# First layer of a hybrid decoder trunk: weight rests of three input units on GpSimd, convolution tap matrices on ScalarE, 12 instead of 15 taps per channel chunk on TensorE

## What is computed

```python
h = rms_norm(x, mix_norm[layer])
z = h @ ab_w_in[j]                       # 1024 x 2560
q, k, v, u = jnp.split(z, [512, 1024, 1536], axis=-1)
a = diff_attention(q, k, v, ...)         # 4 heads, two softmaxes each, their difference weights v
c = conformer_conv(u, ...)               # GLU, causal depthwise convolution of width 31 over 512 channels,
                                         # group norm over 64 channels, swish
x = x + jnp.concatenate([a, c], axis=-1) @ ab_w_out[j]
...
# in conformer_conv
val, gate = jnp.split(u, 2, axis=-1)
g = val * jax.nn.sigmoid(gate)
y = lax.conv_general_dilated(g, dw[:, None, :], window_strides=(1,), padding=[(30, 0)], ...) + dw_bias
```

## Time and profile before

| | before |
|---|---|
| median of 3 runs | 1492.41 us |
| the profiled execution: its time | 1492.52 us |
| the profiled execution: its span | 1490.4 us |
| TensorE busy | 1463.7 us (98%) |
| VectorE busy | 1208.6 us (81%) |
| ScalarE busy | 995.7 us (67%) |
| GpSimd busy | 132.8 us (9%) |
| granted TensorE clock, mean | 0.998 |

### The profile page before, as it was taken

One profiled execution on the slowest core, in us unless ns is written; L12 is line 12 of the kernel. 1 busy time (PEld: TensorE's weight loads), 2 busy tenths in 40 slices (PEclk: granted clock), 3 DMA queues, 4 the chain that ended last, 5 costly groups with the idle time before them and its releaser, 6 DMA issues.

```text
span 1490.4 us, 19624 instructions
## 1 busy us (share of the span) xinstructions
PE 1463.7 (98%) x7818; PEld 1237.3 (83%) x7818; DVE 1208.6 (81%) x1031; ACT 995.7 (67%) x850; POOL 132.8 (9%) x201
## 2 busy tenths in 40 slices
PE   8999999999999999999999999999999999999998
PEld 7967888889998778888888888888888888888776
DVE  7976766666386799888888888888888888888997
ACT  5667444465546677777777777777777777777774
POOL 8505200000253000000000000000000000000200
PEclk9999999999999999999999999999999999999999
DMA  9504555546510399999999999999999999999994
GB/s 344 171 6 164 197 197 181 185 143 197 193 34 31 116 349 372 352 387 379 348 377 382 351 374 388 365 362 386 374 349 389 377 349 380 381 347 377 411 377 164
DMA packets 206919, 432.50 MB, mean 290 GB/s; under 512 B 6914, under 2 KB 56251, under 8 KB 206827
## 3 DMA queue, kind: packets, MB, share of 16 engines
q1 hardware_dynamic: 204880, 424.78, 78.2%
q0 software_dynamic: 1904, 6.46, 1.1%
q10 hardware_dynamic: 42, 0.01, 0.0%
HBM read 426.51 MB, written 4.72 MB: 289 GB/s over the span
## 4 chain that ended last, share of the span: by engine, by line
PE 92%; DVE 4%; ACT 2%; issue 1%; DMA 0%; DVEq 0%; SPq 0%; ACTq 0%
PE bank L1466 25%; PE bank L1468 25%; PE bank L1467 25%; PE bank L1507 6%; PE bank L1509 3%; PE bank L1739 2%; PE bank L1868 2%; PE bank L1820 1%; DVE w_l L294 1%; PE bank L1720 1%; DMA raw<-in_ab_w_in 0%; PE bank L1721 0%; ACT w_h L289 0%; PE bank L1567 0%; PE bank L1473 0%
## 5 line engine op out<-in xcount | busy, mean ns | idle before, releaser
L294 DVE TENSOR_TENSOR w_l<-raw,w_h 128x2048 fp32r<-128x2048 f32 x402 | 920.8, 2292 | 182.1 <-ACT w_h L289 181.4
L289 ACT ACTIVATE w_h<-raw 128x2048 fp32r<-128x2048 f32 x402 | 770.9, 1918 | 353.3 <-PE bank L1468 287.4
L1466 PE MATMUL bank<-w_h,hs_h 128*128 128x512 f32 x896 | 355.3, 397 | 3.7 <-DVE w_l L294 2.8
L1468 PE MATMUL bank<-w_h,hs_l 128*128 128x512 f32 x896 | 349.7, 390 | 0.0
L1467 PE MATMUL bank<-w_l,hs_h 128*128 128x512 f32 x896 | 349.0, 390 | 0.0
L1466 PEld LDWEIGHTS bank<-w_h,hs_h 128*128 128x128 f32 x896 | 168.3, 188 | 38.1 <-issue 3.3
L1468 PEld LDWEIGHTS bank<-w_h,hs_l 128*128 128x128 f32 x896 | 168.2, 188 | 36.0
L1467 PEld LDWEIGHTS bank<-w_l,hs_h 128*128 128x128 f32 x896 | 168.5, 188 | 33.2
L1466 PE MATMUL bank<-w_h,ma_h 128*128 128x512 f32 x448 | 174.6, 390 | 1.7 <-DVE w_l L294 1.7
L1467 PE MATMUL bank<-w_l,ma_h 128*128 128x512 f32 x448 | 174.3, 389 | 0.0
L1468 PE MATMUL bank<-w_h,ma_l 128*128 128x512 f32 x448 | 174.3, 389 | 0.0
(11 more groups left out here) (298 smaller groups left out, 1661.1 us busy)
## 6 DMA issues: line engine op xcount, KB each, us to landing
raw<-in_moe_w_in SPq DMA_DIRECT2D x224, 1024.0 KB, 5.7
raw<-in_moe_w_out SPq DMA_DIRECT2D x112, 1024.0 KB, 5.4
raw<-in_ffn_w_in SPq DMA_DIRECT2D x22, 1024.0 KB, 5.0
raw<-in_hgrn_w_in SPq DMA_DIRECT2D x16, 1024.0 KB, 5.1
raw<-in_ffn_w_out SPq DMA_DIRECT2D x11, 1024.0 KB, 4.7
raw<-in_ab_w_in SPq DMA_DIRECT2D x10, 1024.0 KB, 11.3
raw<-in_ab_w_out SPq DMA_DIRECT2D x4, 1024.0 KB, 4.8
raw<-in_hgrn_w_out SPq DMA_DIRECT2D x4, 1024.0 KB, 4.9
```

Of the source, the lines that this page charges most:

```text
L289: act.activation(w_h[:, u0 % S, :], raw[:, u0 % R, :], ACT.Copy).then_inc(w_high, 1)
L294: eng.tensor_tensor(w_l[:, u0 % S, :], raw[:, u0 % R, :], w_h[:, u0 % S, :], ALU.subtract).then_inc(w_low, 1)
L1466: pe.matmul(o, a_high, b_high, start=start, stop=False, skip_group_check=True)
L1468: return pe.matmul(o, a_low, b_high, start=False, stop=stop, skip_group_check=True)
```

## The change

It does five things, all in the first layer.

- GpSimd makes no tap matrices. It makes the rests of units 5, 7 and 9 (`POOL_UNITS`) with a semaphore of its own, `w_pool`; VectorE makes the rest of the following unit after it has waited for GpSimd's, and counts both.
- ScalarE makes the tap matrices, now 24, in four goes of six behind the high parts of units 4 to 7.
- PE_TAPS is 12: TensorE has 12 taps for each chunk of pair 1, VectorE 19.
- VectorE has 7 steps of taps ahead of the point where units 5, 7 and 9 stood and 4 elsewhere, taps 0 to 6 of pair 1 ahead of the norms of queries and keys, taps 6 to 8 behind the lambda steps, none within the softmax, and 8 to 19 behind it.
- TensorE has 14 taps ahead of the transposes (22 before), 3 ahead of the mean products (none before) and 7 behind (8 before).

```diff
-PE_TAPS = 15
+PE_TAPS = 12
+POOL_UNITS = (5, 7, 9)
...
+            if isinstance(u0, int) and isinstance(rounds, int) and rounds == 0 and u0 in POOL_UNITS:
+                eng.wait_ge(w_pool, POOL_UNITS.index(u0) + 1)
+            else:
+                eng.wait_ge(w_low, u0 + 1 + R * rounds)
...
+        def split_pool(pool, u0):
+
+            pool.wait_ge(w_high, u0 + 1)
+            pool.tensor_tensor(w_l[:, u0 % S, :], raw[:, u0 % R, :], w_h[:, u0 % S, :], ALU.subtract).then_inc(w_pool, 1)
+
+        def split_after_pool(dve, u0):
+
+            dve.wait_ge(w_pool, POOL_UNITS.index(u0 - 1) + 1)
+            dve.wait_ge(w_high, u0 + 1)
+            dve.tensor_tensor(w_l[:, u0 % S, :], raw[:, u0 % R, :], w_h[:, u0 % S, :], ALU.subtract).then_inc(w_low, 2)
...
-            pool.wait_ge(par_cp, 2)
-            for c in range(2):
-                for k in range(PE_TAPS):
-                    col = (TAPS - PE_TAPS + k) * 4 + 2 + c
-                    pool.tensor_scalar(diag(c * PE_TAPS + k), ident[:], dw[:, col:col + 1], None, ALU.mult).then_inc(c_diag, 1)
+            for u in POOL_UNITS:
+                split_pool(pool, u)
...
-            for u in range(4, N_AB_IN + 1):
-                conv_taps(0, 4 * (u - 4), min(4 * (u - 3), TAPS))
-                split_low(dve, u)
+            at = 0
+            for u in range(4, N_AB_IN):
+                more = 7 if u in POOL_UNITS else 4
+                conv_taps(0, at, min(at + more, TAPS))
+                at += more
                 if u == 5:
                     conv_value(1)
-            conv_taps(0, 28, TAPS)
-            conv_taps(1, 0, 2)
+                if u - 1 in POOL_UNITS:
+                    split_after_pool(dve, u)
+                elif u not in POOL_UNITS:
+                    split_low(dve, u)
+            conv_taps(1, 0, 4)
+            split_after_pool(dve, N_AB_IN)
+            conv_taps(1, 4, 6)
...
+            conv_taps(1, 6, 8)
+
...
             row_max(1)
-            conv_taps(1, 2, 4)
             row_max(2)
-            conv_taps(1, 4, 6)
             row_max(3)
             weights(0, p_0)
             row_max(4)
             row_max(5)
-            conv_taps(1, 6, 8)
...
+            def tap_matrices(n0, n1):
+
+                act.wait_ge(par_cp, 2)
+                for n in range(n0, n1):
+                    col = (TAPS - PE_TAPS + n % PE_TAPS) * 4 + 2 + n // PE_TAPS
+                    act.activation(diag(n), ident[:], ACT.Copy, scale=dw[:, col:col + 1]).then_inc(c_diag, 1)
...
                 split_high(act, u + 3)
+                if 1 <= u <= 4:
+                    tap_matrices(6 * (u - 1), 6 * u)
...
-            conv_part(1, 0, 7)
+            conv_part(1, 0, 2)
...
+            conv_part(1, 2, 5)
             for b in range(2):
                 pe.wait_ge(a_sq, b + 1)
...
-            conv_part(1, 7, PE_TAPS).then_inc(c_pe, 1)
+            conv_part(1, 5, PE_TAPS).then_inc(c_pe, 1)
```

More of the change, by code:

```diff
@@ L183, in build @@
         w_high, w_used = sem("w_high"), sem("w_used")
-        w_low = sem("w_low")
+        w_low, w_pool = sem("w_low"), sem("w_pool")
         x_in = [sem(f"x_in{tt}") for tt in range(TT)]
@@ L241, in wait_split @@
         def wait_split(eng, u0, rounds=0):
-            eng.wait_ge(w_low, u0 + 1 + R * rounds)
+            if isinstance(u0, int) and isinstance(rounds, int) and rounds == 0 and u0 in POOL_UNITS:
+                eng.wait_ge(w_pool, POOL_UNITS.index(u0) + 1)
+            else:
+                eng.wait_ge(w_low, u0 + 1 + R * rounds)
         def level_of(t, g, li):
```

## The result

| | before | changed |
|---|---|---|
| median of the runs | 1492.41 us (1492.30 to 1493.67, 5 runs) | 1500.71 us (1498.17 to 1507.72, 5 runs) |
| profiled execution | 1492.52 us | 1498.17 us |
| span | 1490.4 us | 1496.4 us |
| mean granted clock | 0.998 | 0.997 |

The ratio is 1.0053, 95% interval 1.0037 to 1.0069: slower by 0.5%. In the profiled executions the change costs 5.65 us, in the medians 8.3. The prediction of 1496.9 had the sign right and the range of 1491.7 to 1499.0 did not reach 1500.71.

What follows compares the result with a forecast made beforehand. TensorE, without gaps from 112 us on, carries earlier changes to the end; before that VectorE has next to nothing to spare. +7.0 - 0.3 - 3.6 + 1.3 = +4.4 us gave 1496.9 us, range 1491.7 to 1499.0.

Steps and rivals of the forecast that it cites:

- The bound: From 112 us on TensorE has no gaps, so any gain or loss before that carries to the end one for one.
- Step 1, the matrices: Tap matrices on ScalarE cost 0; taking them off GpSimd gives VectorE back 1.2 us.
- Step 2, the block: GpSimd's rests of units 5, 7, 9 spare VectorE 6.8 us but block its taps 3.9 each, +11.7.
- Side by side: Rival: GpSimd's long subtractions do not hold VectorE's second input; -0.4 us, 1492.1; chance 0.28 including a short block.
- GpSimd starves: Rival: GpSimd gets in only between VectorE's taps, 13.4 us a unit; +6.5 us, 1499.0; chance 0.08.
- The new waits: VectorE's subtractions of units 6, 8, 10 and SyncE's loads wait for GpSimd; loads cost 0, GpSimd is done long before.
- Step 3, the keys: VectorE's order with four more taps ahead of the query and key norms: keys ready at 82.0, +7.0 us.
- TensorE's stands: TensorE stands about 2.8 us ahead of unit 6 and about 2 at unit 8, inside the keys' +7.0.
- The test that I had set myself: If taps are long but TensorE never stands ahead of units 6 and 8, the ledger of VectorE is wrong.
- Step 4, the softmax: Softmax without taps between: first maximum 2.2 us behind the keys, -0.3; first maximum to weights 10.7, -3.6.
- Step 5, the tail: Three TensorE taps ahead of the mean products: +1.3 us to the attention norm, about 1.4 of VectorE idle left.
- The clock: TensorE waits of 2 to 3 us could lower its granted clock; given no case of its own.

Runs made afterwards that it cites:

- x3_matrices_act: Kernel before with only its 30 tap matrices moved from GpSimd to ScalarE; median 1493.18 us, ratio 1.0002.
- x1_rests_back: Changed kernel with the rests of units 5, 7 and 9 made by VectorE again; median 1492.12 us, ratio 0.9992.
- x4_tap_from_psum: Changed kernel with taps 4 to 10 of the first pair taking their accumulator from PSUM instead of SBUF; median 1495.35 us, ratio 1.0021.
- y2_warm_both: Changed kernel with 21 empty matmuls on TensorE ahead of unit 8 and 12 ahead of the scores; median 1498.19 us, ratio 1.0026.
- x2_warm8: Changed kernel with 21 dummy matmuls on TensorE ahead of unit 8 only; median 1499.17 us, ratio 1.0039.
- z2_pieces: Changed kernel with each of GpSimd's three subtractions cut into eight of 256 columns; median 1498.28 us, ratio 1.0029.
- z3_one_unit: Changed kernel with only unit 7's rest on GpSimd, those of 5 and 9 on VectorE; median 1495.55 us, ratio 1.0015.

## Why the prediction was right or wrong

**The bound: right.** In the profiled executions all but 0.1 us of the difference is made ahead of the scan entry and carried to the end one for one.

**Step 1, the matrices: cost right, relief misread.** ScalarE's 30 matrices cost nothing. The 1.2 us given back to VectorE are worth nothing that the marker can tell when they stand alone (`x3_matrices_act`): VectorE waits for ScalarE instead.

**Step 2, the block: mechanism right, size a little low.** 4.4, 4.3 and 4.3 us of subtractions of 4.8 to 4.9 (the second without its own 2 us of waiting), where I took 3.9 of 4.4: 13.0 in all instead of 11.7. The reading that something is free of the block was right, 0.5 us for each, and the mistake was to size the subtraction too short: 4.8 instead of 4.4. "Side by side" is excluded by `x1_rests_back` and `x4_tap_from_psum`. "GpSimd starves" did not occur; GpSimd got in for the whole instruction, and even in pieces its eighth ended after 7.2 to 8.7 us. The new waits cost nothing, as said: GpSimd's 6.86 at unit 7 was over well before the next subtraction.

**Step 3, the keys: right, partly by cancellation.** 82.46 against 82.0. Without the blocks they would have been at 77.1 by my ledger and were at 75.87 in `x1_rests_back`. Of these 1.2 us 0.8 were there already at the rest of unit 4 (29.17 against 29.98 in the kernel before), part of it the later start of that one execution, and 0.2 are idle time that the added taps filled. They made up for the blocks' 1.3 by luck.

**TensorE's stands: wrong in place.** I had it stand 2.8 us ahead of unit 6 and about 2 ahead of unit 8. It never stood at unit 6: VectorE, which began its 14 taps 0.7 us sooner than I had it, took that subtraction at 45.20, just ahead of GpSimd's block though GpSimd's row starts 0.11 earlier. The margin was narrow but the same in each profile of the changed kernel. The block moved behind it and unit 8 took all of it, 5.32 us. The test that I had set myself ("TensorE never stands ahead of units 6 and 8") is half met.

**Step 4, the softmax: one half right.** First maximum to weights fell by 3.44 (3.6 forecast). Keys to first maximum did not fall by 0.3 but rose by 1.04. `y2_warm_both` shows that this is the clock: with it kept, the distance is 2.19, as forecast 2.2.

**Step 5, the tail: right within 0.5.** +0.85 instead of +1.3; 0.72 us of VectorE's idle time were left ahead of the norm, where I had 1.4.

**The step that failed** is "The clock": "Waits of 2 to 3 us on TensorE could let its granted clock fall. In 74 to 112 it was 1.00 through a wait of 1.76. I give it no case of its own." The clock was put at nothing in the sum and in the range. With both waits filled (`y2_warm_both`) the first layer lost 4.4 to 4.8 us where the sum had 4.4, and the median was 1498.19, inside the range. With it the profiled run lost 5.9, and the changed kernel's 14 executions ran from 1497.97 to 1507.72 us, half of them over 1500, while none of the 15 with unit 8's wait filled took over 1499.72. The range's upper end came from GpSimd starving and had no room for a loss that differs from run to run. A row of a wait of 1.76 without a fall said nothing about one of 5.3, and my own sum of stands contained nearly 5 us.

A second, smaller miss is the base. I took the kernel before at 1492.4 to 1492.5; its 101 later runs have medians of 1493.4 to 1494.0.

By medians of runs taken side by side, the 8.3 us are 4.15 of ledger (1498.19 with the waits filled, 1494.04 before), 2.3 of clock (1500.47 against 1498.19), 1.6 of the low draw for the kernel before (1494.04 against 1492.41), and 0.2 between the two medians of the changed kernel. That the ledger comes so near to the forecast of 4.4 is partly the cancellation under step 3.

## What to carry to other kernels

Here work moved to GpSimd was free for VectorE only where VectorE's instructions beside it had one tensor input in SBUF. With two, price it at nearly the whole GpSimd instruction against what VectorE would have needed (here 4.3 lost for 2.28 gained), and don't hope for gaps from cutting it up. When an edit makes TensorE stand, add the clock behind the stand as a case of its own, and look at the spread of the runs, not only at the best profile. A marker behind the edited stage, such as a table load on ScalarE, tells a gain of half a us where the total scatters by 4; take it from two executions of the same kernel before you read less into it.

## What I had not expected of the hardware

The granted clock fell to its lower level behind waits of TensorE of 1.80, 2.76, 3.66, 3.96 and 5.32 us in this stage (for the keys in `x1_rests_back`, `x2_warm8`, `z2_pieces` and `z3_one_unit`, ahead of unit 8 in the changed kernel). Yet it kept 1.00 behind 1.76 and 1.82 ahead of the convolution's means in either kernel, and even behind 2.94 ahead of unit 8 in `z2_pieces`. So in this stage the length of the wait alone does not tell whether the clock falls. With the same wait of 5.3 us the low level lasted between about 3 and about 7 us in different executions. In one execution a first fall led to a second by making the next wait longer.

The block works both ways: GpSimd's second subtraction lasted 6.86 instead of 4.8 us beside VectorE's own of 2.28, which started 0.11 us behind it. Taps that started 0.33 and 0.24 us behind GpSimd's first and third were shut out for the whole rest of them. And the block is per instruction: eight pieces of a subtraction and taps of 0.4 us took turns, with no tap over 0.97 us.
